# The value product of an attention in rounded halves from the second token tile on, and a reordered first tile

## The chip, the cores and the metric

The kernel runs on one core of one Trainium2 chip. The metric is the time of one execution on the device, in microseconds (us); lower is better. Engines are named as the profile names them: PE (TensorE, matmuls) with PEld (its weight loads), DVE (VectorE), ACT (ScalarE), POOL (GpSimd) and SP, which here only issues transfers between the chip's memory and the on-chip buffers.

## What is computed

One layer, 2048 prompt tokens and 8 sample sequences of 8 new tokens with 2048 cached positions each. Cut to what matters here:

```python
qg = q.reshape(b, t, N_KV_HEADS, N_HEADS // N_KV_HEADS, HEAD_DIM)
logits = jnp.einsum('btkgd,btnkd->btkgn', qg, k_sel) * (HEAD_DIM ** -0.5)
logits = jnp.where(valid[:, :, None, None, :], logits, NEG_INF)   # the 256 keys an indexer chose
p = jax.nn.softmax(logits, axis=-1)
o = jnp.einsum('btkgn,btnkd->btkgd', p, v_sel)
...
branch_b = attend(q, qi, wi, k, v, ki) * jax.nn.silu(z_b)
merged = sigmoid(g_a) * (branch_a @ w_pa) + sigmoid(g_b) * (branch_b @ w_pb)
y = x + gate * (merged @ w_out)
```

All tensors are float32. There are 8 query heads, 2 key/value heads and a head size of 128.

## The kernel before

The 2048 prompt tokens are worked off in four tiles of 512 tokens (`t` = 0 to 3); the 64 sample tokens go along with tile 0. A tile is: 17 projections (`PROJ_A`), during which the indexer's scores are made; 64 more (`PROJ_B`), during which DVE picks the keys by bisection; the attention; 8 products `pb` and 8 products `wo`. Each product is a series of matmuls in the type fp32r, with each operand split into a rounded high half and a low half (high·high, high·low, low·high).

**Attention of tiles 1 to 3.** A tile has 16 units, four blocks of 128 queries times four pairs of heads; a unit of block `blk` sees `n = 4t + blk + 1` blocks of 128 keys, so 5 to 8 in tile 1, 9 to 12 in tile 2 and 13 to 16 in tile 3. Summed over the 48 units these are 504 key blocks. In the order of PE's code, unit `u` goes like this. `head_logits(u+1)` makes the next unit's logits, in runs of up to 512 keys, three fp32r matmuls each, into a ring of three PSUM banks that DVE frees (`mask_logits`: scale, add the mask, take the maximum, write `LP`). ACT takes the exponential in place. `turn_p` transposes the probabilities, two key blocks (a group `c`) at a time, into a ring of three PSUM banks, with plain float32 matmuls against `ident`. They are copied to a ring of three buffers `T` (`copy_p` on ACT; from the fourth group on a copy on DVE, except in the units that have late mask work). `group_values` then multiplies: the probabilities stand still, the values `V` stream, in plain float32, one matmul of 128 columns per head and key block:

```python
for hh in range(2):
    ins_ = mm(ps[acc_bank(t, u)][:, hh * HD:(hh + 1) * HD], PT[t][p_slot(t, u, c)][:, (2 * kk + hh) * P:(2 * kk + hh + 1) * P],
              V[:, k, (pr // 2) * HD:(pr // 2 + 1) * HD], k == 0 and hh == 0, k == n - 1, skip_group_check=True)
```

The sum has queries on partitions; DVE's `scale` divides by the row sums into `OB`, PE's `turn_out` transposes it in the next unit, and DVE's `finish` multiplies by the gate `SZB` into `BB`. Each engine works strictly in the order in which its code is written, and semaphores join the engines. `head_values` puts the transposition of group `c+1` ahead of the values of group `c`.

In tile 3, units 0 to 7 also end with `choose` on DVE, a chain of six operations over up to 512 scores that makes a run of the mask of blocks 2 and 3 (`late_runs`).

**Attention of tile 0** (`both_attentions`) is a hand-written series of steps that interleaves the prompt's 16 small units with the sample sequences' attention: page keys are transposed (`keys`, out of `sPG`), copied by ACT and DVE in turn to `sKPT`, multiplied with the queries; the sample mask is added by a matmul of the selector `sSEL` with the rows `sBIAS`, read with a stride of 16 elements (`by_slot`); `values` multiplies cached values in four parts, each part behind one transposition of keys.

**SP** issues transfers in one written order; before `pb` it has already asked for the weights of the first three of these products.

Of the kernel before, what the change touches and what calls it, by code (L numbers as in the profile page):

```python
# [37 lines left out]
P = 128  # L38
# [21 lines left out]
ACT_COPIES = 3  # L60
LATE_COPIES = SEQ // (2 * P)
# [49 lines left out]
def program(nc, ins, outs, plan):  # L111
# [74 lines left out]
    U = own("U", [P, TILE + 2])  # L186
# [99 lines left out]
    sBIAS = at("sBIAS", [NS, PAST + NS], F32R, rS + 8192 + 4352)  # L286
# [16 lines left out]
    sXR = at("sXR", [NS, D], F32, rM + 4096)  # L303

# [62 lines left out]
    def page_free(engine, n):  # L367
# [44 lines left out]
    qk, logits, row_max, expd, p_t, p_copy, p_copy_a, pv, scaled, turned, attn_z = (  # L412
        signal(n) for n in ("qk", "logits", "row_max", "expd", "p_t", "p_copy", "p_copy_a", "pv", "scaled", "turned", "attn_z"))
    k_high, k_split, k_whole = (signal(n) for n in ("k_high", "k_split", "k_whole"))
    q_high, q_split = signal("q_high"), signal("q_split")
    gb_out, gb_in = signal("gb_out", 16), [signal(f"gb_in{i}", 16) for i in range(2)]
    bb_high, bb_low_pool, bb_low_dve = signal("bb_high"), signal("bb_low_pool"), signal("bb_low_dve")
# [12 lines left out]
    ma_scratch = nc.dram_tensor("ma_scratch", [TILES, KC, P, TILE], F32).ap()  # L430
    w_scratch = nc.dram_tensor("w_scratch", [WEIGHTS, P, 2 * KC * P], F32).ap()
# [24 lines left out]
    on_act = lambda t, u, c: c < (LATE_COPIES if late_runs(t, u) else ACT_COPIES)  # L456
# [3 lines left out]
    p_copied = lambda t, u, c: (p_copy_a if on_act(t, u, c) else p_copy).at(t, u, c)  # L460
# [36 lines left out]
    def _(sp):  # L497
# [61 lines left out]
        def store_a(t, i):  # L559
# [10 lines left out]
            if n == "v":  # L570
                sp.wait_ge(*a_done.at(t, i, "P"))
                sp.dma_start(outs["v_prompt"][0, 0, r, f].rearrange("(b p) d -> p b d", p=P),
                             V[:, BLOCKS * t:BLOCKS * (t + 1), f * HD:(f + 1) * HD]).then_inc(*v_out.mark(t, f))
# [7 lines left out]
            if t == 0 and n == "ki":  # L581
                sp.wait_ge(*a_done.at(t, i, "S"))
                sp.dma_start(outs["kidx_sample"][0].rearrange("s t d -> (s t) d"), sKIO[:, :]).then_inc(*s_out.mark(n))

# [21 lines left out]
        for t in range(TILES):  # L606
# [10 lines left out]
            for i in range(len(PROJ_B)):  # L617
                j = first + len(PROJ_A) + i
                if j + 3 not in AFTER_PAGES:
                    load_w(j + 3)  # L620
                if j + 2 not in AFTER_PAGES:
                    store_w(j + 2)
# [24 lines left out]
            if t == 0:  # L647
                store_w(AFTER_PAGES[0])
                store_w(AFTER_PAGES[1])
            sp.wait_ge(*(k_whole.at(t) if t + 1 < TILES else qk.at(t, len(UNITS) - 1)))  # L650
# [17 lines left out]
            for f in range(KC):  # L668
# [12 lines left out]
                if f >= 2:  # L681
                    store_y(t, f - 2)
            for f in range(KC - 2, KC):
                store_y(t, f)
# [14 lines left out]
    def _(act):  # L699
# [60 lines left out]
        def evac_a(t, i, j):  # L760
            n, f = PROJ_A[i]
            for p in parts(t):
# [5 lines left out]
                if n == "q" and p == "P":  # L768
# [5 lines left out]
                    elif t and f == 0:  # L774
                        act.wait_ge(*k_out.at(t - 1, 1))
                    act.activation(paired(t, QSQ[f % 4][:, :]), src, ACT.Square).then_inc(*evac.mark(j, p))
# [146 lines left out]
        def masks(t):  # L923
# [3 lines left out]
            if t == 0:  # L927
                act.wait_ge(*mask.at(t, "S"))
                act.activation(sBIAS[:, :], sSC[:, :], ACT.Copy, scale=-NEG).then_inc(*biased.mark(t, "S"))
# [32 lines left out]
        def both_attentions():  # L962
            sample_keys_copy(0, 0, 0)
            sample_keys_copy(0, 0, 2)
            for s in range(len(UNITS) + LEAD + 2):
# [9 lines left out]
                if in_units(k):  # L975
                    exponentials(0, k)
                if s == len(UNITS) + LEAD:
# [8 lines left out]
                if after[0] in PAIRS:  # L986
                    sample_keys_copy(*after, 2)
# [33 lines left out]
        def copy_p(t, u, c):  # L1021
            n = BLOCKS * t + UNITS[u][0] + 1
            act.wait_ge(*p_t.at(t, u, c))
            if u == 0 and c == 0:
# [5 lines left out]
            act.activation(PT[t][p_slot(t, u, c)][:, 0:m], ps[bank("tr", t, u, c)][:, 0:m], ACT.Copy  # L1030
                           ).then_inc(*p_copy_a.mark(t, u, c))

        def attend(t):
            for u in range(len(UNITS) + 1):
# [108 lines left out]
    def _(pe):  # L1143
# [229 lines left out]
        def both_attentions():  # L1373
# [24 lines left out]
            def logits(u, c):  # L1398

                claim(0)  # L1400
                if (u, c) == (0, 0):
                    pe.wait_ge(*biased.at(0, "S"))
                rows = by_slot(sBIAS[:, 0:PAST])[:, 4 * c:4 * c + 4, :] if c < 4 else sBIAS[:, PAST:PAST + NS]
                n = TILE if c < 4 else NS
                mm(ps[0][:, 0:n], sSEL[u // 2][:, u % 2, :], rows, True, False, skip_group_check=True)
# [46 lines left out]
            for s in range(len(UNITS) + LEAD + 1):  # L1452
# [18 lines left out]
                for x in range(4):  # L1471
                    if x == 2 and in_units(k - 1) and unit_groups(0, k - 1) > 1:
                        turn_p(0, k - 1, 1, 3)
                    if after[0] in PAIRS:
                        keys(*after, x)
# [9 lines left out]
        def turn_p(t, u, c, b=None):  # L1485
# [12 lines left out]
            freed[b] = p_copied(t, u, c)  # L1498
# [42 lines left out]
        def group_values(t, u, c):  # L1541
# [4 lines left out]
            pe.wait_ge(*p_copied(t, u, c))  # L1546
            if c == 0:
                claim(acc)
            for kk in range(min(2, n - 2 * c)):
                k = 2 * c + kk  # L1550
                for hh in range(2):
                    ins_ = mm(ps[acc][:, hh * HD:(hh + 1) * HD], PT[t][p_slot(t, u, c)][:, (2 * kk + hh) * P:(2 * kk + hh + 1) * P],
                              V[:, k, (pr // 2) * HD:(pr // 2 + 1) * HD], k == 0 and hh == 0, k == n - 1, skip_group_check=True)
# [3 lines left out]
        def head_values(t, u):  # L1557

            groups = unit_groups(t, u)
            if u == len(UNITS) - 1:  # L1560
                for hh in range(2):
                    pe.wait_ge(*expd.at(t, u, hh))
                turn_p(t, u, 0)
# [961 lines left out]
```

## Time and profile before

| | before |
|---|---|
| median of 3 runs (range) | 3245.71 us (3241.59 to 3247.2) |
| time of the profiled execution | 3244.32 us |
| span of the profiled execution | 3242.5 us |
| PE busy | 3164.9 us, 98% of the span |
| DVE, ACT, POOL busy | 58%, 34%, 26% |
| mean granted PE clock | 0.996 of full |

The profile is of one execution; its time is its span and 1.8 us around it. A matmul's listed duration includes the time in which it drains while the next one runs already, so what a series of matmuls costs is read from one start to the next, not from the durations. The rows that the prediction rests on stand further below.

### The profile page before, as it was taken

How to read it: one execution, taken by the hardware profiler on the slowest of the kernel's cores; microseconds unless marked ns; L12 is line 12 of the kernel's file. 1: busy time of each engine (PE TensorE's matmuls, PEld its weight loads, DVE VectorE, ACT ScalarE, POOL GpSimd, SP SyncE). 2: the span in 40 equal slices, each digit the busy share in tenths (PEclk: the TensorE clock that was granted, in tenths of full speed). 3: DMA queues.
4: the chain of work that ended last, by engine and by line, in shares of the span. 5: the costliest groups of instructions: out<-in, count | busy, mean ns of one | idle time of the engine just before them, and what ended most of it. 6: DMA issues, size and time to landing. Idle time of an engine off the chain costs nothing.

```text
span 3242.5 us, 48134 instructions
## 1 busy us (share of the span) xinstructions
PE 3164.9 (98%) x18999; PEld 2745.4 (85%) x18999; DVE 1879.8 (58%) x3640; ACT 1100.5 (34%) x1956; POOL 839.2 (26%) x765
## 2 busy tenths in 40 slices
PE   7999999999899999999999999999999999999999
PEld 6999999956888888888887888889888788889987
DVE  5443695044535993035257999056437899947652
ACT  3444332345324221154244221154226322135431
POOL 2345675444510332012200331100310133010011
PEclk9999999999999999999999999999999999999999
DMA  8765678674874555622744556610563455650017
GB/s 299 252 213 197 223 274 288 242 250 153 295 236 156 198 193 207 233 97 77 255 160 154 195 192 210 229 35 11 201 212 120 158 195 198 218 187 11 9 37 238
DMA packets 262353, 592.52 MB, mean 183 GB/s; under 512 B 17485, under 2 KB 174343, under 8 KB 212466
## 3 DMA queue, kind: packets, MB, share of 16 engines
q1 hardware_dynamic: 251620, 551.57, 50.0%
q0 software_dynamic: 10368, 37.75, 3.5%
q8 instruction: 152, 2.49, 0.3%
q14 instruction: 71, 0.58, 0.1%
q10 hardware_dynamic: 142, 0.13, 0.0%
HBM read 448.93 MB, written 140.47 MB: 182 GB/s over the span
## 4 chain that ended last, share of the span: by engine, by line
PE 91%; DVE 3%; ACT 2%; DMA 1%; POOL 1%; issue 1%; ACTq 0%; SPq 0%; DVEq 0%; POOLq 0%
PE ps L1162 84%; PE ps L1167 7%; DMA WR<-in_w_proj_b 1%; DVE RS L1828 1%; POOL BBL L2425 0%; DMA GB<-gb_scratch 0%; DVE XN L1749 0%; ACT SC L921 0%; DVE LP L2090 0%; POOL WLH L2264 0%; DVE OB L2101 0%; DMA WR<-in_w_in 0%; DMA ST<-in_state_conv 0%; DVE sKPT L2014 0%; ACT JUNK L733 0%
## 5 line engine op out<-in xcount | busy, mean ns | idle before, releaser
L1162 PE MATMUL ps<-HTH,WLH 128*128 128x512 f32 x3504 | 1128.0, 390 | 0.0
L1162 PEld LDWEIGHTS ps<-HTH,WLH 128*128 128x128 f32 x3504 | 657.9, 188 | 139.2 <-issue 5.0
L1162 PE MATMUL ps<-HTL,WLH 128*128 128x512 f32 x1752 | 682.0, 389 | 0.0
L1961 DVE TENSOR_SCALAR_CACHE_REDUCE JUNK<-SC,SMALL 128x384 bf16<-128x384 f32 (+13 forms) x392 | 580.0, 1479 | 15.6 <-POOL sSC L2350 1.7
L1162 PE MATMUL ps<-H,WLH 128*128 128x288 f32 x3504 | 483.8, 299 | 4.8 <-DVE H L1788 2.0
L1162 PEld LDWEIGHTS ps<-H,WLH 128*128 128x128 f32 x3504 | 474.2, 191 | 6.7 <-issue 2.4
L1162 PEld LDWEIGHTS ps<-HTL,WLH 128*128 128x128 f32 x1752 | 329.1, 188 | 65.3
L2090 DVE CUSTOM_DVE_ANT_0 LP<-ps,SC,RQ 128x512 f32<-128x512 f32 (+3 forms) x320 | 201.7, 667 | 294.1 <-ACT SC L921 277.6
L885 ACT ACTIVATE T<-ps 128x512 f32<-128x512 f32 x192 | 115.0, 599 | 701.5 <-PE ps L1162 698.1
L2264 POOL TENSOR_TENSOR WLH<-WR,WLH 128x1024 fp32r<-128x1024 f32 x97 | 236.2, 2435 | 319.4 <-ACT WLH L708 319.3
L1162 PE MATMUL ps<-V,T 128*128 128x128 f32 x2016 | 263.9, 276 | 0.8 <-ACT T L1030 0.8
L1900 DVE SCALAR_TENSOR_TENSOR SC<-T,WI,SC 128x512 f32<-128x512 f32 (+3 forms) x266 | 180.1, 702 | 117.9 <-ACT T L819 117.1
L1162 PEld LDWEIGHTS ps<-V,T 128*128 128x128 f32 x2016 | 243.8, 192 | 3.3 <-ACT T L1030 2.0
L819 ACT ACTIVATE T<-ps 128x512 f32<-128x512 f32 (+3 forms) x304 | 162.3, 546 | 172.7 <-PE ps L1162 157.9
L1030 ACT ACTIVATE T<-ps 128x512 f32<-128x512 f32 (+1 forms) x176 | 103.2, 588 | 257.6 <-PE ps L1167 257.4
L708 ACT ACTIVATE WLH<-WR 128x1024 fp32r<-128x1024 f32 x97 | 102.8, 1060 | 247.1 <-DMA WR<-in_w_in 177.7
L1167 PE MATMUL ps<-ident,LP 128*128 128x128 f32 x1088 | 166.7, 274 | 3.8 <-ACT LP L1018 3.8
L2412 POOL TENSOR_TENSOR QLOW<-QU,QHIGH 128x256 fp32r<-128x256 f32 x64 | 46.9, 736 | 423.3 <-ACT QHIGH L1011 423.1
L1018 ACT ACTIVATE LP<-LP,SMALL 128x128 f32<-128x128 f32 (+15 forms) x128 | 152.3, 1195 | 0.8 <-DVE SMALL L2095 0.7
L1167 PEld LDWEIGHTS ps<-ident,LP 128*128 128x128 f32 x1088 | 127.8, 141 | 21.9 <-issue 12.5
L1162 PE MATMUL ps<-KHIGH,QHIGH 128*128 128x512 f32 (+3 forms) x320 | 127.3, 398 | 3.0 <-DVE SMALL L2090 2.8
L1162 PE MATMUL ps<-MGH,WLH 128*128 128x512 f32 x384 | 124.4, 395 | 0.9 <-POOL MGL L2431 0.9
(344 smaller groups left out, 4544.2 us busy)
## 6 DMA issues: line engine op xcount, KB each, us to landing
WLH<-w_scratch SPq DMA_DIRECT2D x291, 1024.0 KB, 4.8
w_scratch<-WLH SPq DMA_DIRECT2D x97, 1024.0 KB, 5.7
WR<-in_w_in SPq DMA_DIRECT2D x73, 512.0 KB, 4.3
MW<-in_w_mod SPq DMA_DIRECT2D x6, 2048.0 KB, 16.2
q_scratch<-QO SPq DMA_DIRECT2D x32, 256.0 KB, 5.6
ma_scratch<-T SPq DMA_DIRECT2D x32, 256.0 KB, 5.6
gb_scratch<-GB SPq DMA_DIRECT2D x32, 256.0 KB, 5.6
QU<-q_scratch SPq DMA_DIRECT2D x64, 128.0 KB
```

Of the source, the lines that this page charges most:

```text
L708: act.activation(WH[j % 3][:, :, :], WR[j % 3][:, :, :], ACT.Copy).then_inc(*w_high.mark(j))
L819: act.activation(T[1 + r % 4][:, 0:n], ps[bank("idx", t, b, h, c)][:, 0:n], ACT.Relu).then_inc(*relu.mark(r))
L885: act.activation(paired(t, dst), src, func).then_inc(*evac.mark(j, p))
L1018: act.activation(row, row, ACT.Exp, bias=NM[:, u % 2, hh:hh + 1], accum_out=SUM[:, u % 2, hh:hh + 1]).then_inc(*expd.mark(t, u, hh))
L1030: act.activation(PT[t][p_slot(t, u, c)][:, 0:m], ps[bank("tr", t, u, c)][:, 0:m], ACT.Copy).then_inc(*p_copy_a.mark(t, u, c))
L1162: return pe.matmul(out, lhsT, rhs, start=start, stop=stop, **more)
L1167: return pe.transpose(out, in_, ident[a:a + n, a:a + n])
L1900: dve.scalar_tensor_tensor(dst, x, w, dst, ALU.mult, ALU.add).then_inc(*scored.mark(r))
L1961: ins_ = dve.tensor_scalar(JUNK[0:n, 0:row.shape[1]], row, MID[0:n, c:c + 1], 0.0, ALU.is_ge, ALU.add, accum_out=CNT[0:n, c:c + 1])
L2090: ins_ = dve.tensor_tensor_reduce(LP[t][:, u % 2, hh, c:c + n], ps[bank("qk", t, u, hh, c)][:, 0:n], scores(t)[:, blk, c:c + n], RQ[:, blk ...
L2264: pool.tensor_tensor(WL[j % 3][:, :, :], WR[j % 3][:, :, :], WH[j % 3][:, :, :].bitcast(F32), ALU.subtract).then_inc(*w_split.mark(j))
L2412: pool.tensor_tensor(QLOW[u % 2][:, :, :], QU[u % 2][:, :, :], QHIGH[u % 2][:, :, :].bitcast(F32), ALU.subtract).then_inc(*q_split.mark(t, u))
```

## The change

From tile 1 on the value product is turned round. The values stand still, as a rounded half `VR` and the rest `VL`, and the transposed probabilities of two heads stream as 256 columns, as a rounded half `PTH` and the rest `PTL`; a key block takes three fp32r matmuls (`VR`·`PTH`, `VR`·`PTL`, `VL`·`PTH`). The sum then has the head's channels on partitions, so it need not be transposed, and the division by the row sums is done by two matmuls of `ones` with a diagonal matrix `DG` (`lengths`), whose result DVE multiplies with the gate. ACT makes `PTH` of every group. DVE makes `PTL` from PSUM, but for groups 3 and 7 of units 0 to 13 ACT makes a second copy `PTW` and POOL subtracts (`low_on_pool`). POOL also makes `DG`, and the halves of the values behind the projections. `VL` passes through the chip's memory and lies in two weight buffers during the attention, so the weights of `pb` 1 and 2 are asked for only after the last value product. The diff shows SP, ACT, PE, DVE and POOL in this order. In tile 0 the mask rows become five separate contiguous pieces, written by ACT behind the first two key copies; and PE's step runs all four parts of `values` in one stretch between the second and the third transposition of keys.

```diff
+    low_on_pool = lambda t, u, c: c % 4 == 3 and u < len(UNITS) - 2
+    p_low = lambda t, u, c: (p_low_pool if low_on_pool(t, u, c) else p_low_dve).at(t, u, c)
...
+                if t and h >= 0 and BLOCKS * (t + 1) > 8 * h:
+                    load_vl(t, h)
+                elif j + 3 not in AFTER_PAGES:
                     load_w(j + 3)
...
+                sp.wait_ge(*pv.at(t, len(UNITS) - 1))
+                for h in range(2):
+                    if BLOCKS * (t + 1) > 8 * h:
+                        load_w(first + len(PROJ_A) + len(PROJ_B) + 1 + h)
...
+            act.activation((PTH if t else PT[t])[slot][:, 0:m], src, ACT.Copy).then_inc(*p_copy_a.mark(t, u, c))
+            if t and low_on_pool(t, u, c):
+                act.activation(PTW[slot][:, 0:m], src, ACT.Copy).then_inc(*p_raw.mark(t, u, c))
...
+                    mm(out, VR[:, k, head], PTH[slot][:, cols], k == 0, False, skip_group_check=True)
+                    mm(out, VR[:, k, head], PTL[slot][:, cols], False, False, skip_group_check=True)
+                    ins_ = mm(out, VL[t][k // 8][:, k % 8, head], PTH[slot][:, cols], False, k == n - 1, skip_group_check=True)
...
+            turn_p(t, u, 1)
             for c in range(groups):
-                if c + 1 < groups:
-                    turn_p(t, u, c + 1)
+                if c + 2 < groups:
+                    turn_p(t, u, c + 2)
+                if last and c == groups - 1:
+                    lengths(t, u)
                 group_values(t, u, c)
...
+            dve.tensor_tensor(PTL[slot][:, 0:m], ps[bank("tr", t, u, c)][:, 0:m], PTH[slot][:, 0:m].bitcast(F32), ALU.subtract
+                              ).then_inc(*p_low_dve.mark(t, u, c))
...
+                link(dve.tensor_tensor(halves(TB[u % 2][:, :]), right, gate, ALU.mult))
+                right, gate = left, halves(TB[u % 2][:, :])
...
+                link(dve.tensor_copy(R4R[u % 2][:, 0:2], RIN[:, u % 2, :]))
+                dve.tensor_tensor(R4[u % 2][:, 2:4], RIN[:, u % 2, :], R4[u % 2][:, 0:2], ALU.subtract).then_inc(*scaled.mark(t, u))
...
+                for c in (1, 2):
+                    probabilities_low(t, u, c)
                 unit_sum(t, u)
                 if u:
                     finish(t, u - 1)
-                    dve.tensor_copy(PT[t][p_slot(t, u, c)][:, 0:m], ps[bank("tr", t, u, c)][:, 0:m]).then_inc(*p_copy.mark(t, u, c))
+                for c in range(3, groups):
+                    probabilities_low(t, u, c)
                 for b, r in late_runs(t, u):
                     choose(t, scores(t)[:, b, 0:width(BLOCKS * t + b)], P, b, b, r)
-                scale(t, u)
...
+                    for c in range(unit_groups(t, u)):
+                        probabilities_low(t, u, c)
+                        if c == min(3, unit_groups(t, u) - 1):
+                            diagonals(t, u)
                     if u == len(UNITS) - 2 and t + 1 < TILES:
                         whole_keys(t)
```

The order of instructions, first on PE in a unit of tile 2 with ten key blocks, from the last transposition (`ident`,`LP`) on. Before:

```order
L1167 MATMUL ps<-ident,LP 128x128 [waits p_copy_a]
L1167 MATMUL ps<-ident,LP 128x128 x3
L1162 MATMUL ps<-V,T_102 128x128 [waits p_copy]
L1162 MATMUL ps<-V,T_102 128x128 x3
L1162 MATMUL ps<-V,T_100 128x128 [waits p_copy]
L1162 MATMUL ps<-V,T_100 128x128 x3
```

After, from the same transposition on, down to the group that POOL prepares:

```order
L1229 MATMUL ps<-ident,LP 128x128 [waits p_low_dve]
L1229 MATMUL ps<-ident,LP 128x128 x3
L1224 MATMUL ps<-PTH_244,VR 128x256 [waits p_low_dve]
L1224 MATMUL ps<-PTL_250,VR 128x256
L1224 MATMUL ps<-PTH_244,VL_231 128x256
L1224 MATMUL ps<-PTH_244,VR 128x256
L1224 MATMUL ps<-PTL_250,VR 128x256
L1224 MATMUL ps<-PTH_244,VL_231 128x256
L1224 MATMUL ps<-PTH_245,VR 128x256 [waits p_low_pool]
```

Four matmuls of 128 columns per group became six of 256; the transpositions now run two groups ahead instead of one; and the values wait for a subtraction on DVE (`p_low_dve`) or POOL (`p_low_pool`) where they waited for a copy. On DVE, in tile 3, from the end of a unit's logits to the next unit's (the ISA rows are `mask_logits`; `GT` to `SC` is `choose`). Before:

```order
L2095 TENSOR_REDUCE SMALL<-SMALL 128x1 [waits logits]
L2114 RECIPROCAL SMALL<-SMALL 128x2 [waits expd]
L2108 TENSOR_TENSOR BB<-ps,SZB 128x2x128 [waits turned,dve_step]
L1990 TENSOR_SCALAR GT<-SC,SMALL 128x512
L1991 SCALAR_TENSOR_TENSOR BD<-SC,SMALL,GT 128x512 [waits dve_step]
L1992 SCALAR_TENSOR_TENSOR PFX<-BD,SMALL 128x512 [waits dve_step]
L1994 COPY SMALL<-PFX 128x1 [waits dve_step]
L1995 SCALAR_TENSOR_TENSOR BD<-PFX,SMALL,BD 128x512 [waits dve_step]
L1996 SCALAR_TENSOR_TENSOR SC<-BD,GT 128x512 [waits dve_step]
L2101 TENSOR_SCALAR OB_115<-ps,SMALL 128x128 [waits pv,dve_step]
```

After, in the first such unit, which has no `finish` yet (in the others its two products stand behind the `R4R` rows), down to the start of `choose`:

```order
L2208 TENSOR_REDUCE SMALL<-SMALL 128x1 [waits logits]
L2186 TENSOR_TENSOR PTL_250<-ps,PTH_244 128x512 [waits p_copy_a]
L2186 TENSOR_TENSOR PTL_251<-ps,PTH_245 128x512 [waits p_copy_a]
L2234 RECIPROCAL SMALL<-SMALL 128x2 [waits expd]
L2236 CAST R4R_252<-SMALL 128x2 [waits dve_step]
L2237 TENSOR_TENSOR R4R_252<-SMALL,R4R_252 128x2 [waits dve_step]
L2186 TENSOR_TENSOR PTL_250<-ps,PTH_244 128x512 [waits p_copy_a]
L2186 TENSOR_TENSOR PTL_251<-ps,PTH_245 128x512 [waits p_copy_a]
L2186 TENSOR_TENSOR PTL_249<-ps,PTH_243 128x256 [waits p_copy_a]
L2091 TENSOR_SCALAR GT<-SC,SMALL 128x512
```

Five subtractions now stand between the logits and `choose`, a sixth among the logits, where before these units had none of the copies on DVE: `choose` has moved from beside PE's value products to behind the last of their inputs.

## Rows read from the trace of the kernel before

**Rows 1.** The page's first part: busy us, share, instructions of each engine.

```profile
PE 3164.9 (98%) x18999; PEld 2745.4 (85%) x18999; DVE 1879.8 (58%) x3640; ACT 1100.5 (34%) x1956; POOL 839.2 (26%) x765
```

**Rows 2.** PE's timeline in tile 1 (n=6): start us, duration us, instruction.

```profile
1445.87 0.48 PE L1162 MATMUL ps<-KHIGH,QHIGH 128*128 128x512 f32 x1
1446.19 0.39 PE L1162 MATMUL ps<-KLOW,QHIGH 128*128 128x512 f32 x1
...
1446.66 0.28 PE L1162 MATMUL ps<-KHIGH,QHIGH 128*128 128x256 f32 x1
...
1447.01 0.39 PE L1162 MATMUL ps<-KHIGH,QHIGH 128*128 128x512 f32 x1
...
1448.85 0.60 PE L1167 MATMUL ps<-ident,LP 128*128 128x128 f32 x4
1449.29 1.06 PE L1162 MATMUL ps<-V,T 128*128 128x128 f32 x8
1450.18 0.60 PE L1167 MATMUL ps<-ident,LP 128*128 128x128 f32 x4
```

**Rows 3.** ACT's timeline in the same unit.

```profile
1444.31 0.60 ACT L1030 ACTIVATE T<-ps 128x512 f32<-128x512 f32 x1 [0.73 <-PE ps L1167]
1444.80 0.93 ACT L1018 ACTIVATE LP<-LP,SMALL 128x768 f32<-128x768 f32 x1
...
1449.49 0.60 ACT L1030 ACTIVATE T<-ps 128x512 f32<-128x512 f32 x1 [0.42 <-PE ps L1167]
```

**Rows 4.** Groups of DVE and POOL by form, whole span.

```profile
L1917 DVE TENSOR_TENSOR sKPL<-ps,sKPH 128x512 fp32r<-128x512 f32 x32 | 21.8, 685 | 34.2 <-ACT sKPH L905 34.2
...
L2431 POOL TENSOR_TENSOR MGL<-T,MGH 128x512 fp32r<-128x512 f32 x24 | 31.8, 1326 | 101.4 <-DVE MGH L2159 101.4
...
L2407 POOL TENSOR_TENSOR KT<-KLOW,KHIGH 128x256 f32<-128x256 f32 x8 | 5.5, 724 | 11.1 <-PE ps L1162 11.1
```

**Rows 5.** DVE's timeline in one late unit of tile 3 (n=13).

```profile
2934.36 0.75 DVE L2090 CUSTOM_DVE_ANT_0 LP<-ps,SC,RQ 128x512 f32<-128x512 f32 x1
...
2936.85 0.75 DVE L2090 CUSTOM_DVE_ANT_0 LP<-ps,SC,RQ 128x512 f32<-128x512 f32 x1
...
2939.62 0.42 DVE L2108 TENSOR_TENSOR BB<-ps,SZB 128x256 f32<-128x256 f32 x1
2939.96 0.48 DVE L1990 TENSOR_SCALAR GT<-SC,SMALL 128x512 f16<-128x512 f32 x1
...
2947.49 0.61 DVE L2101 TENSOR_SCALAR OB<-ps,SMALL 128x128 f32<-128x128 f32 x2 [3.24 <-PE ps L1162]
```

**Rows 6.** The chain that ended last, tile 3: one such piece per unit.

```profile
2952.94 0.66 PE ps L1167 x6
...
2966.85 0.66 PE ps L1167 x6
...
2981.49 0.66 PE ps L1167 x6
```

**Rows 7.** PE's timeline at the start of tile 0's attention.

```profile
643.77 1.06 PE L1167 MATMUL ps<-ident,sPG 128*128 128x128 f32 x8 [3.27 <-ACT sKPT L941]
644.76 0.67 PE L1162 MATMUL ps<-sBIAS,sSEL 64*128 64x512 f32 x1
645.36 2.17 PE L1162 MATMUL ps<-sKPT,sQ 128*32 128x512 f32 x8
```

**Rows 8.** The chain that ended last, a step of tile 0's attention.

```profile
687.25 0.69 DVE sKPT L2014
...
688.51 0.44 PE ps L1167 x2
```

**Rows 9.** Transfers by kind: count, KB each, median us from issue to landing.

```profile
WLH<-w_scratch SPq DMA_DIRECT2D x291, 1024.0 KB, 4.8
...
XN<-in_x_prompt SPq DMA_DIRECT2D x3, 2048.0 KB, 8.0
```

**Rows 10.** A POOL subtraction that runs beside one on DVE, by form.

```profile
L2425 POOL TENSOR_TENSOR BBL<-BB,BBH 128x512 fp32r<-128x512 f32 x12 | 19.1, 1623 | 65.5 <-PE ps L1162 65.5
```

More of the change, by code:

```diff
@@ L926, in masks, with sample_mask @@
                     block_mask(t, b)
[L927 to L929 removed]
+        def sample_mask():
+            act.wait_ge(*mask.at(0, "S"))
+            for c in range(5):
+                if c < 4:
+                    dst, src = sBIAS[c][:, :].rearrange("t (i q) -> t i q", i=4), by_slot(sSC[:, 0:PAST])[:, 4 * c:4 * c + 4, :]
+                else:
+                    dst, src = sBIAS[c][:, :], sSC[:, PAST:PAST + NS]
+                act.activation(dst, src, ACT.Copy, scale=-NEG).then_inc(*biased.mark(0, "S", c))
         def sample_keys_copy(u, c, g):
@@ L1470, in both_attentions @@
                     turn_probabilities(u - 1, c)
-                for x in range(4):
+                if after[0] in PAIRS:
+                    keys(*after, 0)
+                    if in_units(k - 1):
+                        group_values(0, k - 1, 0)
+                    keys(*after, 1)
+                    if late[0] in PAIRS:
+                        for x in range(4):
+                            values(*late, x)
+                    keys(*after, 2)
+                    if in_units(k - 1) and unit_groups(0, k - 1) > 1:
+                        turn_p(0, k - 1, 1, 3)
+                    keys(*after, 3)
+                    if in_units(k - 1) and unit_groups(0, k - 1) > 1:
+                        group_values(0, k - 1, 1)
+                for x in range(0 if after[0] in PAIRS else 4):
                     if x == 2 and in_units(k - 1) and unit_groups(0, k - 1) > 1:
                         turn_p(0, k - 1, 1, 3)
-                    if after[0] in PAIRS:
-                        keys(*after, x)
                     if late[0] in PAIRS:
@@ L2088, in mask_logits @@
                 for x, (c, n) in enumerate(runs):
+                    if t and u and hh and x == len(runs) - 1:
+                        probabilities_low(t, u - 1, 0)
                     dve.wait_ge(*qk.at(t, u, hh, c))
@@ L2454, in _ @@
                     gather_index_keys(i // 2 + 2)
+                if t and i == 0:
+                    value_halves(t, 0)
+                    value_halves(t, 1)
                 if i == (SAMPLE_ITEMS + 3 if t == 0 else 1):
```

187 lines of the change are left out of this document (141 added, 46 removed).

## The prediction

> **What bounds the kernel now.** The page's first part comes first: PE is busy for 98% of the span [rows 1], so a saving counts where it shortens PE's row of matmuls, and a new wait counts where it stops that row. Then PE's timeline in an ordinary unit, read from start to start: eight value instructions, which are two key blocks, take 0.89 us (1449.29 to 1450.18), so 0.445 us a block; four transpositions take 0.44 (1448.85 to 1449.29); three fp32r matmuls of 256 columns take 0.35 (1446.66 to 1447.01) and one of 512 takes 0.235 (half of 1446.19 to 1446.66), but the first one behind plain float32 values takes 0.32 (1445.87 to 1446.19), 0.07 to 0.09 more [rows 2]. Last DVE in a late unit of tile 3: its logits, its mask chain and an idle time of 3.24 us before `OB` [rows 5]. That slack is what the change spends.
>
> **PE's saving.** A key block falls from 0.445 to 0.35 us: 504 blocks by 0.095 are 47.9 us. Logits behind fp32r values no longer pay the 0.07, 48 times: 3.4. `lengths` (two matmuls of 256 columns, 0.23) stands where two transpositions (0.22) stood. The saving is 51.3 us if nothing waits. In transposition-then-value order I add no 0.09, since the four transpositions and that price together are the 0.44 that I count anyway. The bounds: a block costs no less than 0.35, which is a row for the same three matmuls of 256 columns, and at worst it keeps its 0.445 and nothing is saved.
>
> **Group 3 and group 7, by way of POOL.** A piece now goes transposition, `PTH` on ACT, `PTW` on ACT, subtraction on POOL, PE. ACT starts 0.20 us after the transpositions' last start (1449.29 to 1449.49), a second ACT operation follows the first after 0.49 (1444.31 to 1444.80) and takes 0.60 [rows 3]; POOL's subtraction of this size takes 1.33 [rows 4]; with two semaphores that is 2.7 us. PE in the meantime has two groups of values at 0.70 and up to two sets of transpositions at 0.44: 2.28 us for n from 12 on, 2.06 for n=11, 1.84 for n=10, 1.62 for n=9, and only the values, 1.40, where the group is the unit's last (n=8; n=16's group 7). PE so waits 0.4, 0.65, 0.85, 1.1 and 1.3 us. Half-sized last groups (n=7, n=15) need about 1.7, with the 0.72 of POOL's operation on 256 columns [rows 4], and wait 0.3. Units 14 and 15 leave it to DVE, but behind `unit_sum` and `finish`, which for n=8 costs about the same 1.3. Outside the late units this sums to 4 x 0.3 (n=7), 4 x 1.3, 4 x 1.1, 4 x 0.85, 4 x 0.65, 2 x 0.4 (n=12), 4 x 0.7 (n=15) and 2 x 1.7 (n=16): 23.6 us. Bounds: nothing, if PE comes later anyway, and 30.
>
> **The eight late units of tile 3.** A unit now takes 13.9 us at n=13 (2952.94 to 2966.85) and 14.6 at n=14 [rows 6]. Before, `choose` (2939.96 to 2944.25, 4.3 us) ran beside PE's values, and DVE was still idle for 3.24 us. Now it stands behind the last subtraction, and PE can run only three runs of logits ahead of it. The loop that results is: `choose` 4.3; the first head's logits 2.5 (2934.36 to 2936.85); the second head's up to its last run 2.05 [rows 5]; the subtraction of group 0, 0.69 [rows 4] and a wait for its copy, 0.8; then PE from the values of group 0 to the last transposition, four groups at 0.70, transpositions of 1.54 and POOL's 0.4, 4.75; and the last group's copy and subtraction, two thirds of 0.60 and 0.69 and the start, 1.05. Sum 15.45, so 1.5 us more than now; at n=14 both sides grow by 0.7. Lost are 8 x 1.5 and the 10.8 us that PE's saving had for these units (4 x 1.3 and 4 x 1.4): 22.8 us. Bounds: DVE without any wait has 5.0 of logits, six subtractions of 3.9, some 1.4 of small things and `choose` 4.3, 14.6 us, so 0.7 lost a unit, 16.4 in all; and 30, if `choose` finds still more in its way.
>
> **Small units of tile 1.** At n=5 DVE has about 2.3 us of logits, 1.7 of subtractions, an estimated 0.6 for the sums and 0.8 for `finish` (two products of 0.42 [rows 5]), 5.4 us before any wait, against PE's 5.2 or so after the saving; its subtractions stand one behind the other in front of PE. I take n=5 to keep nothing of its 0.55 us and n=6 to keep 0.3 of 0.64: 3.6 us lost (bounds 0 and 8).
>
> **Moved transfers and POOL's queue.** The weights of `pb` 1 and 2 are asked for after the last value. A transfer of 1 MB lands after 4.8 us and one of 2 MB after 8.0 [rows 9], so 1.6 and 3.2 a MB. PE wants `pb` 1 some 7 us after the last value (1.5 until `pb` 0 starts, 24 matmuls at 0.235): hidden. Everything behind it on SP's queue comes later too: two gates (0.5 MB), the next tile's tokens (2 MB), `ma` (0.25 MB) and `pb` 3 (1 MB). In tile 2 that is 5.75 MB, landing at 20.0 against a want at 18.4: 1.6 us. In tile 1 only one weight moved, in tile 3 no tokens follow: hidden. `VL` itself loads beside the first logits; the storing of `VL` and POOL's `value_halves` lie beside 64 products and are costed at nothing, some 4 us if that cover were gone. POOL's `whole_keys`, eight additions (0.72 each in tile 1 [rows 4]), now stands between the diagonals of units 14 and 15, and `lengths` of unit 15 waits for it: about 2 us in tile 1 (bounds 0 and 4), hidden in tile 2, where the units are longer.
>
> **Tile 0.** The 16 matmuls with 512 mask columns take 0.60 us each now (644.76 to 645.36) [rows 7]; as contiguous rows I take the 0.32 of rows 2, so 4.5 us less (bounds 0 and 5.8). The first key copy no longer waits for the whole mask: of the 3.27 us [rows 7] I take 1.1 back, the rest being block masks and the copy itself (bounds 0 and 2). The value stretch saves changes between transpositions and small matmuls, but the last part of `values` then no longer covers the copy (0.69) and `OB` that the next step's PE waits for (687.25 to 688.51) [rows 8]: nothing either way, bounds 3 us each. Together 5.6 us less.
>
> **Sum.** -51.3 + 23.6 + 22.8 + 3.6 + 1.6 + 2.0 - 5.6 = -3.3 us on the profiled execution's 3244.3, so 3241; the median of the runs shown is 1.4 higher, so 3242 in its terms.
>
> **A rule against it.** POOL's subtraction takes 1.33 us with DVE elsewhere [rows 4] and 1.62 where DVE subtracts from on-chip memory at the same time [rows 10], so the two can hinder each other. The Trainium skill, "SBUF — State Buffer", section "SBUF: two separate sides", says that DVE and POOL share a pair of ports as an exclusive lock, taken by a DVE operation with two inputs from that memory against a POOL operation that reads it. The row agrees in direction. By this rule DVE's new subtractions, with one input in PSUM, go free, and the sum stays; but `choose` has three such operations, and POOL's new work may meet them.
>
> **Rivals.**
> - **The saving shows** (3205 to 3232, about 3217). If ordinary waits are half of mine (12) and the late loop shrinks to DVE's own work (16.4 instead of 22.8), with some 3 us less in the small terms, 25 us come off. For it: DVE, ACT and POOL are busy for 58, 34 and 26% only [rows 1]. Against: the path over POOL is a latency, not a load.
> - **Slower: the hand-over of each group becomes the bound** (3252 to 3275). 264 groups went from one copy to a copy and a subtraction before PE may go on. A wait of 0.1 us at each beyond those counted adds 26 us, 3268; it decides from (6.5 + 3.3) / 264 = 0.04 us on. For it: DVE is at 90% and more of PE's time in the small units. Against: transpositions now run two groups ahead.
> - **Slower by the shared ports**: if one POOL operation of 1.33 us comes in the way of `choose` in each late unit, 8 x 1.33 = 10.6 us are added, 3253. This is the skill's rule at work in this kernel; rows 10 show it for another pair.
> - **The change doesn't do what it says**: value blocks stay at 0.445 because the two sides' weight loads bound them; then the 48 us fall out, 3290.
>
> **Chances.** Forecast, the waits eat the saving (3233 to 3251): 0.45. Saving shows: 0.25. Hand-over: 0.2. Shared ports: 0.05. No saving: 0.05. A measurement of this kernel can tell about 0.2%, 6.5 us. Below 3239 lie the second case and a third of the first: faster 0.4; above 3252 the last three: slower 0.3; the same 0.3. The range that leaves out 2 in 10 goes from 3212 to 3266.
>
> **What would show it.** PE's value matmuls 0.115 us apart in pairs of key blocks; PE waiting for POOL's `PTL`, longest in n=8 and n=9 units; late units of about 15.4 us with PE idle at the fourth run of logits, behind `choose`; 0.3 us between the mask matmul and the next in tile 0. Wrong would be most likely the late loop or POOL's path, which carry 46 us between them.

## The result, and the profile after

The changed kernel takes 3269.53 us (median of 7 runs, 3257.96 to 3273.27) against 3245.71 (7 runs, 3241.16 to 3247.24): it is slower, by a ratio of 1.0073 (95% interval 1.0063 to 1.0082), 23.8 us. The profiled execution, the slowest of the seven, took 3273.27 us, with a span of 3270.7 and a mean granted clock of 0.990 (0.989 to 0.994 over the seven); before, 3242.5 and 0.996.

The page's first part, which answers to [rows 1]:

```profile
PE 3152.3 (96%) x18495; PEld 2720.2 (83%) x18495; DVE 1964.9 (60%) x3824; ACT 1164.9 (36%) x2088; POOL 951.9 (29%) x871
```

PE has less to do and is busy for less of a longer span, so it waits more. For whom, its list of waits says (us in total, how often, the longest):

```profile
PE ps L1224 <- DVE SMALL L2203: 19.5, 11, 2.5
PE ps L1224 <- POOL PTL L2533: 12.6, 22, 1.1
...
PE ps L1224 <- DVE PTL L2186: 5.0, 15, 0.8
```

The first line is PE at its logits, waiting for `mask_logits` to free a bank; before, it was 2.8 us. Where the time went is read from each tile's attention, from its first logits to the first matmul of `pb`:

| | before | after | difference | priced in the prediction |
|---|---|---|---|---|
| tile 0, and all up to tile 1's first logits | 1404.5 | 1403.6 | -0.9 | -5.6 |
| attention of tile 1 | 118.6 | 122.1 | +3.5 | +1.0 |
| attention of tile 2 | 184.0 | 183.8 | -0.2 | -5.9 |
| attention of tile 3 | 247.5 | 269.9 | +22.4 | +5.8 |
| all the rest | 1287.9 | 1291.3 | +3.4 | +1.6 |

The differences sum to +28.2 where the priced ones sum to -3.1, so 31.3 us are to be explained, and tile 3 holds 16.6 of them. Here is one late unit of 13 key blocks on PE (start, duration, instruction); its period is read from one `lengths` (`DG`) to the next:

```profile
2934.04 0.69 PE L1224 MATMUL ps<-DG,ones 128*128 128x256 f32 x2
...
2943.95 0.39 PE L1224 MATMUL ps<-KHIGH,QLOW 128*128 128x512 f32 x1
2946.80 0.33 PE L1224 MATMUL ps<-KHIGH,QHIGH 128*128 128x128 f32 x1 [2.46 <-DVE SMALL L2203]
...
2948.31 0.63 PE L1224 MATMUL ps<-KHIGH,QHIGH 128*128 128x512 f32 x1
2948.74 0.63 PE L1224 MATMUL ps<-KLOW,QHIGH 128*128 128x512 f32 x1
...
2951.96 0.45 PE L1224 MATMUL ps<-DG,ones 128*128 128x256 f32 x2
```

The period is 17.92 us; it was 13.9 [rows 6], and the prediction had 15.4. PE runs three runs of logits, waits 2.46 us at the fourth, as foretold, and 1.5 us later its matmuls of 512 columns start 0.43 us apart instead of 0.235: the lower of the clock's two levels, 1.2 GHz. The granted clock of that stretch is 0.50 (window, its length, busy us and instructions of PE, PEld, DVE, ACT and POOL, granted clock, DMA share, GB/s):

```profile
2948.40:2950.80 2.40, 2.40 (x7) 1.80 (x7) 1.67 (x5) 0.00 (x0) 0.00 (x0) 0.50 0.00 0
```

DVE in the same unit, and POOL beside its end:

```profile
2940.92 0.42 DVE L2186 TENSOR_TENSOR PTL<-ps,PTH 128x256 fp32r<-128x256 f32 x1 [0.41 <-ACT PTH L1092]
2941.26 0.48 DVE L2091 TENSOR_SCALAR GT<-SC,SMALL 128x512 f16<-128x512 f32 x1
...
2944.86 1.09 DVE L2097 SCALAR_TENSOR_TENSOR SC<-BD,GT 128x512 f32<-128x512 f16 x1
2945.99 0.75 DVE L2203 CUSTOM_DVE_ANT_0 LP<-ps,SC,RQ 128x512 f32<-128x512 f32 x1
```

```profile
2944.60 0.81 POOL L2573 TENSOR_TENSOR QLOW<-QU,QHIGH 128x256 fp32r<-128x256 f32 x1 [4.36 <-ACT QHIGH L1072]
```

The chain from `GT` to `SC` stands between the last subtraction and the next logits and takes 4.69 us (4.3 before). The granted clock by windows, before and after:

```profile
640.00:660.00 20.00, 14.68 (x85) 7.32 (x84) 5.89 (x13) 6.61 (x11) 11.22 (x12) 0.91 0.85 315
...
2920.00:3060.00 140.00, 139.88 (x1041) 129.79 (x1041) 97.67 (x269) 75.03 (x110) 7.37 (x10) 1.00 0.04 11
```

```profile
640.00:660.00 20.00, 15.81 (x62) 7.14 (x61) 4.80 (x9) 8.50 (x14) 10.74 (x12) 0.66 0.79 288
...
1520.00:1540.00 20.00, 17.50 (x76) 14.39 (x75) 10.07 (x16) 5.78 (x11) 10.43 (x8) 0.83 0.71 263
...
2920.00:3060.00 140.00, 121.33 (x761) 104.17 (x759) 116.61 (x279) 68.59 (x107) 26.25 (x26) 0.94 0.03 8
```

A mean of 0.94 over 140 us is up to 8.4 us of full-speed work missing. It isn't spread evenly: in five of the eight late units the granted clock is 0.89 to 0.92 over the unit, in the other three it is 1.00. The 0.83 of 1520 to 1540 us (1.00 before) is up to 3.4 us more, mostly in the table's last row. PE was busy for 139.88 of these 140 us before, and for 121.33 after.

An ordinary unit, of nine key blocks in tile 2, PE:

```profile
2146.65 0.46 PE L1224 MATMUL ps<-DG,ones 128*128 128x256 f32 x2
...
2150.71 0.28 PE L1224 MATMUL ps<-PTH,VL 128*128 128x256 f32 x1
2151.90 0.39 PE L1224 MATMUL ps<-PTH,VR 128*128 128x256 f32 x1 [0.91 <-POOL PTL L2533]
...
2157.21 0.40 PE L1224 MATMUL ps<-DG,ones 128*128 128x256 f32 x2
```

The wait for POOL is 1.07 us from start to start (1.19 less a matmul's 0.12), priced at 1.1. But the unit takes 10.56 us where 9.9 stood before, and the prediction had it 0.2 longer, not 0.6.

At the end of tile 2's attention PE waits for POOL's `BBL`, the low half of the first operand of `pb`; before and after:

```profile
2294.35 0.47 PE L1162 MATMUL ps<-BBH,WLH 128*128 128x512 f32 x1 [0.35 <-POOL BBL L2425]
```

```profile
2298.98 0.47 PE L1224 MATMUL ps<-BBH,WLH 128*128 128x512 f32 x1 [2.00 <-POOL BBL L2586]
```

It is the same in tiles 1 and 3. All waits of PE from the start of a tile's last two units on sum to 3.7 to 4.6 us a tile, and to 2.0 or 2.1 before: some 6 us over three tiles.

Tile 0 after the change, PE and then ACT:

```profile
644.78 0.76 PE L1224 MATMUL ps<-sBIAS,sSEL 64*128 64x512 f32 x1 [1.29 <-ACT sBIAS L989]
...
652.88 3.52 PE L1224 MATMUL ps<-sKPT,sQ 128*32 128x512 f32 x6
...
665.71 0.49 PE L1224 MATMUL ps<-sBIAS,sSEL 64*128 64x512 f32 x1
666.13 1.48 PE L1224 MATMUL ps<-sKPT,sQ 128*32 128x512 f32 x8
```

```profile
643.58 4.08 ACT L989 ACTIVATE sBIAS<-sSC 64x512 fp32r<-64x512 f32 x5
```

A mask row takes 0.42 us (0.60 in [rows 7]). The five pieces take ACT 4.08 us, the one before took 1.95; PE waits for them, then for the key copies behind them, and six products that took 1.08 us before take 3.52 at the lower clock (granted 0.50 from 652 to 656.7 us, 0.66 in the mean of 640 to 660).

### The profile page after: what moved, and what is told of

Same layout as the page of the kernel before. It is cut to its first block, busy times and chain, and to the rows that moved or that the text cites. A ratio compares the mean times of both kernels' runs of the same rounds, so it can differ in the third digit from the quotient of the medians.

```text
span 3270.7 us, 47625 instructions
## 1 busy us (share of the span) xinstructions
PE 3152.3 (96%) x18495; PEld 2720.2 (83%) x18495; DVE 1964.9 (60%) x3824; ACT 1164.9 (36%) x2088; POOL 951.9 (29%) x871
## 4 chain that ended last, share of the span: by engine, by line
PE 81%; issue 6%; ACT 4%; DVE 4%; POOL 2%; DMA 2%; SPq 0%; another core or an unknown queue 0%; DVEq 0%; ACTq 0%; POOLq 0%
PE ps L1224 76%; PE ps L1229 4%; ACT LP L1079 2%; POOL PTL L2533 1%; ACT PTH L1092 1%; DVE PTL L2186 1%; DMA MW<-in_w_mod 1%; DVE LP L2203 1%; DVE RS L1929 1%; DMA WR<-in_w_proj_b 1%; POOL QLOW L2573 0%; DMA GB<-gb_scratch 0%; ACT SC L975 0%; POOL WLH L2385 0%; POOL BBL L2586 0%
## 5 line engine op out<-in xcount | busy, mean ns | idle before, releaser
L1092 ACT ACTIVATE PTH<-ps 128x512 fp32r<-128x512 f32 (+1 forms) x264 | 147.4, 579 | 229.9 <-PE ps L1229 228.5
L1224 PE MATMUL ps<-PTH,VR 128*128 128x256 f32 x504 | 161.4, 320 | 19.5 <-POOL PTL L2533 12.6
L2186 DVE TENSOR_TENSOR PTL<-ps,PTH 128x512 fp32r<-128x512 f32 (+1 forms) x224 | 145.1, 668 | 53.2 <-ACT PTH L1092 50.8
L1229 PE MATMUL ps<-ident,LP 128*128 128x128 f32 x1088 | 160.0, 275 | 7.1 <-ACT LP L1079 7.1
L1224 PE MATMUL ps<-PTL,VR 128*128 128x256 f32 x504 | 141.6, 281 | 0.0
L1224 PE MATMUL ps<-PTH,VL 128*128 128x256 f32 x504 | 141.4, 281 | 0.0
## 6 DMA issues: line engine op xcount, KB each, us to landing
MW<-in_w_mod SPq DMA_DIRECT2D x6, 2048.0 KB, 16.4
```

The source lines that it names most:

```text
L1092: act.activation((PTH if t else PT[t])[slot][:, 0:m], src, ACT.Copy).then_inc(*p_copy_a.mark(t, u, c))
L1224: return pe.matmul(out, lhsT, rhs, start=start, stop=stop, **more)
L1229: return pe.transpose(out, in_, ident[a:a + n, a:a + n])
L2186: dve.tensor_tensor(PTL[slot][:, 0:m], ps[bank("tr", t, u, c)][:, 0:m], PTH[slot][:, 0:m].bitcast(F32), ALU.subtract).then_inc(*p_low_dve. ...
```

## The experiments

**Where does tile 3's time go?** The reason read from the trace (theory A) is the place of `choose`. DVE is idle for 37.85 us ahead of tile 3's attention, so the eight runs can be moved there:

```profile
2906.89 0.75 DVE L2203 CUSTOM_DVE_ANT_0 LP<-ps,SC,RQ 128x512 f32<-128x512 f32 x1 [37.85 <-ACT SC L975]
```

```diff
-                if name not in late_blocks(t):
-                    for r in range(len(pieces(row.shape[1]))):
-                        choose(t, row, n, c, name, r)
+                for r in range(len(pieces(row.shape[1]))):
+                    choose(t, row, n, c, name, r)
...
-                for b, r in late_runs(t, u):
-                    choose(t, scores(t)[:, b, 0:width(BLOCKS * t + b)], P, b, b, r)
```

> The eight runs of the mask chain (choose) of tile 3 move from behind the subtractions of units 0 to 7 to DVE's idle time of 37.85 us ahead of tile 3's attention; nothing is left out. Theory A (the late units' order): units of 13 key blocks fall from 17.9 us to about 13.5 and those of 14 from 18.2 to about 14.3, as the other ordinary units came out 0.4 us below before; tile 3's attention falls by some 30 us and the kernel to about 3239. Theory B (the hand-over of every group is the bound, wherever choose stands): the late units keep 16 us or more, and the kernel stays above 3258.

> The same move of choose in the kernel before. If choose ran there beside the value products, as the prediction reads it, the time stays at 3245 within 4 us. If choose cost something there too, the kernel falls by up to 10 us, and early_choose against after would show a gain that isn't the change's own.

Early_choose takes 3247.56 us (ratio to before 1.0007, 0.9998 to 1.0017), 22 us less than after. Two `lengths` in it, and its first wait in tile 3:

```profile
2908.31 0.47 PE L1224 MATMUL ps<-KHIGH,QHIGH 128*128 128x128 f32 x1 [4.79 <-DVE SMALL L2202]
...
2932.80 0.45 PE L1224 MATMUL ps<-DG,ones 128*128 128x256 f32 x2
...
2946.28 0.46 PE L1224 MATMUL ps<-DG,ones 128*128 128x256 f32 x2
```

The period is 13.48 us, theory A's number, and 14.3 at 14 blocks. The kernel missed 3239 by 8.6 us, of which 3.7 are a late start: the eight runs were a little too long, DVE ended them at 2907.46, and PE waited 4.79 us at the start of tile 3 (1.10 in after). The rest is mainly that not every late unit had lost 4 us. Before_early takes 3249.08 (1.0011, 1.0002 to 1.0021): its late units keep their 13.9 us, and what it loses is the same late start (tile 3's attention 253.3 instead of 247.5). So `choose` was free where it stood, and in after it costs the late units 1.6 to 4.4 us each, 3.3 in the mean of the seven periods.

**Does the clock fall because PE waits?** 

```diff
                     banks["qk", t, u, hh, c] = b
+                    if t == TILES - 1 and 2 <= u <= 9 and not hh and c == 3 * TILE:
+                        spare = 3 + ring["tr"] % 3
+                        pe.wait_ge(*freed[spare])
+                        for i in range(6 if u == 5 else 10):
+                            mm(ps[spare][:, :], QHIGH[u % 2][:, 0, :], KHIGH[:, pr // 2, 0:TILE], True, True)
                     claim(b)
```

> After, with 10 more logits matmuls of 512 columns (2.35 us), whose result nobody reads, put into PE's wait for the fourth run of logits in the late units (6 in the unit with the short chain); the wait itself stays. Theory C (PE's idle time lets the granted clock fall, and the matmuls behind it pay): the granted clock of 2920 to 3055 us goes from about 0.93 to 0.98 or more, the late units get 0.7 to 1.2 us shorter, the kernel falls by 6 to 9 us. Rival (the clock falls for another reason, or the loop is DVE's alone and hides it): the time stays or grows by up to 3 us.

3260.7 us (1.0049, 1.0031 to 1.0066), 9 us less than after with more work. In the traces tile 3's attention takes 6.8 us less (263.1), and 3.6 lie ahead of tile 1's attention, where the two kernels are alike. The same window and two `lengths`:

```profile
2920.00:3060.00 140.00, 137.61 (x874) 118.52 (x873) 120.38 (x294) 74.22 (x114) 26.59 (x26) 1.00 0.03 9
```

```profile
2945.02 0.45 PE L1224 MATMUL ps<-DG,ones 128*128 128x256 f32 x2
2961.50 0.40 PE L1224 MATMUL ps<-DG,ones 128*128 128x256 f32 x2
```

The clock is back at 1.00, the unit at 16.48 us. The units in which the clock had fallen are 1.1 to 1.6 us shorter; the three others take what they took, within 0.2 us. So PE's idle time lets the clock fall, and theory C holds; its cost falls on five of the eight late units.

**Is it POOL's path?** First POOL out of the subtractions, and then, with POOL in, the sums and `finish` behind them.

```diff
-    low_on_pool = lambda t, u, c: c % 4 == 3 and u < len(UNITS) - 2
+    low_on_pool = lambda t, u, c: False
```

> After, with every subtraction on DVE: no second copy on ACT, none on POOL. Theory D (the path over POOL is a latency that DVE hasn't): the waits behind POOL go, tile 2's attention falls from 183.8 to about 173 us, tiles 1 and 2 together by 12, while the late units of tile 3 lose up to 0.7 us each; the kernel falls by 5 to 12 us. Rival (DVE is the bound of ordinary units too): the units of 5 to 9 key blocks get longer and the kernel grows.

```diff
-                for c in (1, 2):
+                early = groups if u < len(UNITS) - 2 else 3
+                for c in range(1, early):
                     probabilities_low(t, u, c)
                 unit_sum(t, u)
                 if u:
                     finish(t, u - 1)
-                for c in range(3, groups):
+                for c in range(early, groups):
                     probabilities_low(t, u, c)
```

> After, with unit_sum and finish behind a unit's last subtraction on DVE (but for the last two units of a tile); POOL keeps its groups, choose stays in the late units. It tells apart what seven_first changed at once. If the place of finish alone held PE up, tile 2's attention falls from 183.8 to about 175 us as in seven_first, and tile 1's by 2. If it is POOL's path that PE waits for (theory D), the units of 9 and 10 key blocks stay at 10.5 and 10.8 and tile 2 within 2 us of 183.8.

Dve_only takes 3259.61 us (1.0042, 1.0028 to 1.0056), 10 less than after: in the traces 6.9 in tile 3's attention (263.0), 4.1 in tile 2's (179.8, short of the 173 expected), and in tile 1's a loss of 3.0; another 4.1 lie ahead of tile 1's attention, where the two kernels are alike. There the units of 7 key blocks went from 7.2 to 7.94:

```profile
1468.06 0.40 PE L1224 MATMUL ps<-DG,ones 128*128 128x256 f32 x2
1476.00 0.40 PE L1224 MATMUL ps<-DG,ones 128*128 128x256 f32 x2
```

Sums_last takes 3297.36 us (1.0148, 1.013 to 1.0167). Tiles 1 and 2 stay as in after (122.2 and 183.8), so as long as POOL has its groups it is POOL's path that PE waits for in ordinary units, and not `finish`. What neither theory foresaw is tile 3: its late units grow to 18.8 to 20.8 us. The sums and `finish`, 1.4 us that had stood in DVE's gaps, now stand in front of the next logits as `choose` does, and the clock falls further (0.85 in 2920 to 3060 us; PE's waits for `SMALL` are 30.7 us).

**Is it the block, or the load?** The six operations of `choose` (as `choice` lists them) in pairs ahead of the subtractions of the fourth group and the next ones. The fourth is POOL's, so DVE runs four of the six ahead of the fifth group's subtraction and two ahead of the sixth's:

```diff
...
+                late = [op for b, r in late_runs(t, u) for op in choice(t, scores(t)[:, b, 0:width(BLOCKS * t + b)], P, b, b, r)]
                 for c in range(3, groups):
+                    for op in late[:2]:
+                        op()
+                    late = late[2:]
                     probabilities_low(t, u, c)
-                for b, r in late_runs(t, u):
-                    choose(t, scores(t)[:, b, 0:width(BLOCKS * t + b)], P, b, b, r)
+                for op in late:
+                    op()
```

> After, with the six operations of choose in the late units put in pairs ahead of DVE's third and later subtractions instead of as a block behind them; nothing is left out and nothing leaves the late units. If the block in front of the next logits is what hurts, the late units fall from 17.9 to about 15.5 us. If it is DVE's load in a unit (logits, subtractions and choose, some 14.6 us without any wait, on a loop that passes through PE twice), delayed subtractions hold up the values and with them the logits behind them, and the units stay at 17 us or more.

3292.23 us (1.0142, 1.0125 to 1.0159); the late units take 18.5 to 20.7 us. PE now waits for the subtractions, and the clock falls to 0.84 in the mean:

```profile
PE ps L1224 <- DVE PTL L2197: 29.2, 31, 2.8
```

```profile
2920.00:3060.00 140.00, 116.14 (x659) 100.67 (x657) 108.27 (x245) 60.25 (x94) 23.48 (x22) 0.84 0.03 7
```

The run isn't a clean test of block against load, since it also brought `choose` beside POOL's work. In six of the eight late units its first two operations, 0.48 and 0.75 us in after, take 1.1 to 1.4 us each while POOL makes `PTL` and `DG`, 8.8 us more in all:

```profile
2956.52 1.42 DVE L2105 TENSOR_SCALAR GT<-SC,SMALL 128x512 f16<-128x512 f32 x1
2957.98 1.41 DVE L2106 SCALAR_TENSOR_TENSOR BD<-SC,SMALL,GT 128x512 f16<-128x512 f32 x1
```

```profile
2956.35 1.30 POOL L2548 TENSOR_TENSOR PTL<-PTW,PTH 128x512 fp32r<-128x512 f32 x1 [12.89 <-ACT PTW L1094]
2957.59 1.25 POOL L2539 TENSOR_TENSOR DG<-ident,R4R 128x512 fp32r<-128x512 f32 x1
```

Of the two orders tried with the whole chain inside the unit, neither helps: behind the subtractions it delays the next logits, between them it delays the values. What of interleave's loss is DVE's load, what POOL and what the clock, was not separated.

**Tile 0's two parts, undone one at a time.**

```diff
...
-                act.activation(dst, src, ACT.Copy, scale=-NEG).then_inc(*biased.mark(0, "S", c))
+            act.activation(sBIAS[:, :], sSC[:, :], ACT.Copy, scale=-NEG).then_inc(*biased.mark(0, "S"))
...
+            sample_mask()
             sample_keys_copy(0, 0, 0)
             sample_keys_copy(0, 0, 2)
-            sample_mask()
...
```

> After, with the sample mask again as one strided piece that ACT writes ahead of the first key copies (the value stretch stays). Theory A: a mask row then takes 0.60 us on PE instead of 0.42, sixteen times (2.9 us), and the first copy waits for the mask again; tile 1's attention starts 2 to 5 us later than in after and the kernel stays or grows by that. Rival: the pieces cost what they bring (ACT takes 4.08 us for the five, 1.95 for one), and nothing that can be told from run to run changes.

```diff
...
-                    if late[0] in PAIRS:
-                        for x in range(4):
-                            values(*late, x)
...
-                for x in range(0 if after[0] in PAIRS else 4):
+                for x in range(4):
                     if x == 2 and in_units(k - 1) and unit_groups(0, k - 1) > 1:
                         turn_p(0, k - 1, 1, 3)
+                    if after[0] in PAIRS:
+                        keys(*after, x)
                     if late[0] in PAIRS:
                         values(*late, x)
```

> After, with the four parts of values each behind a transposition of keys again, and ACT's third key copy in its old place (the mask pieces stay). The prediction put the stretch at nothing: within 3 us of after. Rival: the stretch brings 0.2 us in each of some 16 steps, and without it the kernel grows by 3 us or more.

Old_mask takes 3270.06 us (1.0076) and old_stretch 3268.99 (1.0071): neither can be told from after. In the traces, tile 1's attention starts at 1402.65 and 1406.44 (after 1403.61), while the granted clock of 640 to 660 us is 0.83 and 0.91 (after 0.66), which is up to 5 us of PE's time by itself. One trace of each can't settle a few us here: the eight traced kernels whose tile 0 is that of after start tile 1's attention between 1399.5 and 1406.6. So the pieces bring nothing to be seen, and what the stretch brings stays open.

**A version that beats both.** Seven runs of `choose` early, the last one operation by operation behind the subtractions of units 0 to 4 of tile 3; in seven_pool1 POOL subtracts in tile 1 alone; in seven_first never, with the sums last.

```diff
...
+                runs = len(pieces(row.shape[1]))
+                for r in range(runs - 1 if t == TILES - 1 and name == 3 else runs):
+                    choose(t, row, n, c, name, r)
...
+                if t == TILES - 1 and u < 5:
+                    last_run(t, u)
...
```

> Early_choose with two changes. The last run of the mask chain goes back into tile 3, one operation behind the subtractions of each of units 0 to 4, because all eight together kept DVE busy until 2907.46 and PE waited 4.79 us for its first logits; and POOL subtracts in tile 1 alone, where dve_only was slower (units of 7 and 8 key blocks 0.75 us longer), and DVE in tiles 2 and 3, where it was faster (tile 2 by 4 us, tile 3 by 7). Theory A with D: 4 us less at the start of tile 3, 4 in tile 2, 5 to 7 in tile 3: about 3234. Rival: the five operations delay the subtractions behind them, and the kernel stays at 3247 within 4 us.

> As seven_pool1, but with every subtraction on DVE in all tiles, and with unit_sum and finish behind a unit's last subtraction instead of ahead of the fourth group's (but for the last two units of a tile). If dve_only lost in tile 1 because finish stood ahead of the fourth subtraction, its units of 7 and 8 key blocks fall from 7.94 and 8.24 us to 7.2 and 7.5 or less, and the kernel comes out below seven_pool1 by 3 to 8 us. Rival: DVE's load is the bound there, and they stay at 7.9 and 8.2.

Seven_pool1 takes 3229.9 us (0.9957, 0.994 to 0.9974), seven_first 3223.42 (0.9935, 0.9918 to 0.9952), 21 us less than the runs of before beside it and 46 less than after. In seven_first the attentions of tiles 1 to 3 take 119.8, 174.7 and 235.4 us. Its units of 7 and 8 blocks fell to 7.15 and 7.5, so in dve_only, without POOL, it was the place of `finish`, not DVE's load. This kernel also shows what an ordinary unit of nine blocks costs when PE doesn't wait for POOL:

```profile
2137.83 0.45 PE L1224 MATMUL ps<-DG,ones 128*128 128x256 f32 x2
...
2147.27 0.40 PE L1224 MATMUL ps<-DG,ones 128*128 128x256 f32 x2
2147.50 1.04 PE L1229 MATMUL ps<-ident,LP 128*128 128x128 f32 x8
2148.49 0.38 PE L1224 MATMUL ps<-PTH,VR 128*128 128x256 f32 x1
2148.71 0.28 PE L1224 MATMUL ps<-PTL,VR 128*128 128x256 f32 x1
2148.83 0.28 PE L1224 MATMUL ps<-PTH,VL 128*128 128x256 f32 x1
...
2149.30 0.60 PE L1229 MATMUL ps<-ident,LP 128*128 128x128 f32 x4
2149.68 0.39 PE L1224 MATMUL ps<-PTH,VR 128*128 128x256 f32 x1
...
2152.49 0.40 PE L1224 MATMUL ps<-KHIGH,QHIGH 128*128 128x512 f32 x1
```

And the kernel before, the same stretch of such a unit:

```profile
2150.69 0.60 PE L1167 MATMUL ps<-ident,LP 128*128 128x128 f32 x4
...
2156.16 0.48 PE L1162 MATMUL ps<-KHIGH,QHIGH 128*128 128x512 f32 x1
```

From the first transposition to the next logits it is 4.99 us against 5.47: 0.48 saved by nine key blocks, where the prediction had 9 x 0.095 = 0.86.

## Why the prediction was wrong

It said that waits would eat the saving and put the time at 3242 us; the measured 3269.53 lies above the range. The late units' loop and POOL's path are there as it named them, but the sum under the late loop failed: it left a subtraction out. One mechanism, the clock, had no term, and four more terms were off.

- **The late units** (forecast 15.4 us at n=13, measured 17.92). The loop is right: the last subtraction, `choose`, three runs ahead, the stop at the fourth. The sum under it was added up wrongly: its terms make 16.14, not 15.45, since the first subtraction's 0.69 was dropped; over eight units that is 5.5 us. Busy_wait, at full clock, measures 16.4 to 16.5. The other 1.5 us are the clock, of which the prediction had no term. Against before, the late units cost 23.7 us, where 12 were priced: 11.7 of the 31.3 us.
- **The clock.** Each wait was priced at its own length. Here PE's idle time also lets the clock fall, and the work behind it pays: 6.8 us in tile 3's attention (busy_wait), up to 5 us at the start of tile 0. The mean over the kernel went from 0.996 to 0.990, which is 20 us at most. The Trainium skill says it in "TensorE: Matmul & The Clock Gate", Part 1: the array's clock depends on how busy PE has been. The traces agree (2920 to 3060 us: 1.00 before, 0.94 after, 0.84 in interleave, where PE waits more, and 1.00 again with the wait filled). It is a rule that spoke against this change, and it was missing among the rivals.
- **PE's saving, 51.3 us.** In seven_first units of 9, 10, 11, 12, 15 and 16 blocks save 0.51, 0.56, 0.76, 0.79, 1.11 and 1.18 us, where 0.93, 1.02, 1.12, 1.21, 1.50 and 1.59 were priced (the block's saving and the 0.07). The slope with the blocks is right, 0.095 a block; each unit falls short by about 0.4, whatever its size, which would be some 19 us over 48. Most of it shows in the rows of nine blocks above. By the prediction's own prices the after side's 4.99 us should be 4.69 (14 transpositions at 0.11, nine blocks at 0.35), and 0.21 of the 0.30 between lie at the unit's start. The eight transpositions there take 0.99 us to the first value, 0.11 of it a wait, and that value takes 0.22 instead of 0.12. The prediction added nothing for this first value, since four transpositions and that price together were its 0.44. Four with it measure 0.48 (2149.30 to 2149.68, and 0.10), but the eight measure 1.09, not 0.88.
- **Group 3 and 7 by way of POOL, 23.6 us.** The terms listed make 23.8, and 17.2 were measured: between after and seven_first tile 2 loses 9.1 us (priced 11.2), tile 1 2.3 (6.4 with units of 7 and 8), tile 3's last eight units 5.8 (6.2). Seven_first also moved `finish`, so this is both together.
- **Tile 0, 5.6 us less.** Measured 0.9 less, in a stretch that differs by 7 us between traces of like kernels. The row's cost fell to 0.42 and not to 0.32; the first key copy came earlier, but PE then waited for the pieces. How much the clock took of the rest is not shown.
- **The end of a tile.** Of the 6 us that PE waits more there, the prediction priced 2.0, as a wait for `DG` in tile 1, which measures 0.5; the wait for `BBL` had no term.

**The rivals.** *The hand-over of each group* gave 3252 to 3275, in which the result lies, but not its mechanism: early_choose takes 22 us off without touching one hand-over, and the shortfall of ordinary units goes by the unit, not by the group. *The shared ports* are there, and smaller than priced: `SC<-BD,GT` takes 1.09 us beside POOL's `QLOW` and 0.69 without it, in five of the eight late units, 2.0 us in all. *The saving shows* became true of seven_pool1 and seven_first, once `choose` and most or all of POOL's subtractions were out of the way; its terms make 3221, not 3217. *No saving* is refuted: a block's three matmuls start 0.12 us apart.

## What to carry to other kernels

When an operation moves to an engine, look first at what stands behind it in that engine's order: 4.3 us that cost nothing beside PE's products cost 3.3 us in the mean of the late units, and up to 4.4, once they stood between the last operand and the next logits. Work that nobody waits for belongs into the longest idle time of its engine, here 37.85 us before the tile began, as far as it fits: eight runs ended too late, seven didn't. And a wait of PE that recurs in every unit is to be priced with the slower clock that can follow it, not with its length alone.

## What was not expected of the hardware

- The clock fell though no single wait was longer than 2.5 us in the late units, and came back when 2.35 us of matmuls that nobody reads filled it. In the units in which it fell, slower matmuls, and not the wait, were 1.1 to 1.6 us.
- DVE and POOL hinder each other only in some pairs. DVE's subtraction with one input in PSUM takes 687 ns in the mean and POOL's beside it 1283, no more than the 685 and 1326 of [rows 4]. `SC<-BD,GT`, with no input in PSUM, goes from 0.69 to 1.09 us beside POOL's `QLOW`. That is as the Trainium skill has it ("SBUF — State Buffer", "SBUF: two separate sides"). In the one late unit where `SC<-BD,GT` starts first, it keeps its 0.69 us and `QLOW` takes 1.19 instead of 0.74.
- The same mask written by ACT in five pieces takes 4.08 us instead of 1.95.
